# Token layout of the split moving operands: even and odd tokens of each block of 256 stored apart

## The reference

```python
def _swiglu(x, w_in, w_out):                      # D_FF = 2816, four times
    a, b = jnp.split(x @ w_in, 2, axis=-1)
    return (jax.nn.silu(a) * b) @ w_out
...
z = n @ mix_w_in[l]                               # per layer of the first stack
merged = jax.nn.sigmoid(zga) * (y_a @ proj_a[l]) + jax.nn.sigmoid(zgb) * (y_b @ proj_b[l])
h = h + mod[:, 1, 2] * (merged @ w_out[l])
...
def sq_relu_mlp(h, w_in, w_out):                  # width 4096, three times
    return jnp.square(jax.nn.relu(h @ w_in)) @ w_out
...
qkv = h @ w_qkv                                   # second stack, layer 1
o_lat = o_blocks.transpose(1, 0, 2, 3, 4, 5).reshape(B, L, D) @ w_o
```

## Time and profile before

| | before |
|---|---|
| median of three runs | 3466.84 us |
| range of the runs | 3464.92 to 3466.95 us |
| span of the profiled execution | 3464.7 us |
| TensorE matmul busy | 3413.6 us, 18,494 records |
| TensorE weight loads busy | 2874.5 us |
| VectorE busy | 2165.7 us |
| ScalarE busy | 1318.4 us |
| GpSimd busy | 298.0 us |
| DMA | 452.01 MB, mean 130 GB/s |

### The profile page before, as it was taken

How to read it: one execution, slowest core, us unless ns; L and a number is a source line. 1 busy time by engine, 2 the same in 40 slices (tenths; PEclk the granted TensorE clock), 3 DMA queues, 4 the chain that set the end, 5 groups by cost and what they waited for, 6 DMA issues and landing times.

```text
span 3464.7 us, 46915 instructions
## 1 busy us (share of the span) xinstructions
PE 3413.6 (99%) x18494; PEld 2874.5 (83%) x18494; DVE 2165.7 (63%) x3570; ACT 1318.4 (38%) x1951; POOL 298.0 (9%) x376
## 2 busy tenths in 40 slices
PE   9999999999999999999999999999999999999998
PEld 7888967898888988896789888899988898588888
DVE  7555565656555655666577777888776556655444
ACT  4222463333222422245333523355533236643222
POOL 0000232001000100023100000012100001210000
PEclk9999999999999999999999999999999999999999
DMA  7444302434444344320243444344444311013221
GB/s 279 188 158 163 107 24 101 163 129 168 158 162 151 134 169 158 148 106 12 101 164 140 149 150 170 146 147 182 172 174 165 117 66 68 25 50 112 96 98 48
DMA packets 85561, 452.01 MB, mean 130 GB/s; under 512 B 10304, under 2 KB 12544, under 8 KB 48608
## 3 DMA queue, kind: packets, MB, share of 16 engines
q1 hardware_dynamic: 83168, 439.10, 34.2%
q0 software_dynamic: 2176, 9.92, 0.8%
HBM read 446.88 MB, written 2.10 MB: 130 GB/s over the span
## 4 chain that ended last, share of the span: by engine, by line
PE 84%; DVE 7%; ACT 3%; issue 2%; DMA 2%; POOL 0%; SPq 0%; DVEq 0%; ACTq 0%; POOLq 0%
PE ps L662 21%; PE ps L663 21%; PE ps L664 21%; DVE WL L568 2%; DMA araw<-in_ast 2%; PE ps L2778 1%; PE ps L2780 1%; PE ps L2779 1%; PE ps L3477 1%; PE ps L1039 1%; PE ps L1040 1%; PE ps L1041 1%; ACT P L1859 1%; PE ps L1776 1%; PE ps L1299 1%
## 5 line engine op out<-in xcount | busy, mean ns | idle before, releaser
L662 PE MATMUL ps<-nH,WH 128*128 128x512 f32 x2256 | 880.3, 390 | 0.4 <-ACT rot L3207 0.4
L664 PE MATMUL ps<-nH,WL 128*128 128x512 f32 x2256 | 877.8, 389 | 0.0
L663 PE MATMUL ps<-nL,WH 128*128 128x512 f32 x2256 | 877.8, 389 | 0.0
L568 DVE TENSOR_TENSOR WL<-raw,WH 128x2048 fp32r<-128x2048 f32 (+2 forms) x297 | 651.6, 2199 | 361.5 <-ACT WH L557 360.0
L557 ACT ACTIVATE WH<-raw 128x2048 fp32r<-128x2048 f32 (+2 forms) x299 | 543.2, 1822 | 561.1 <-PE ps L664 479.9
L662 PEld LDWEIGHTS ps<-nH,WH 128*128 128x128 f32 x2256 | 423.5, 188 | 90.6 <-issue 3.3
L664 PEld LDWEIGHTS ps<-nH,WL 128*128 128x128 f32 x2256 | 423.4, 188 | 88.3
L663 PEld LDWEIGHTS ps<-nL,WH 128*128 128x128 f32 x2256 | 423.5, 188 | 87.2 <-issue 0.2
L628 DVE SCALAR_TENSOR_TENSOR araw<-araw,cB 128x1024 f32<-128x1024 f32 x224 | 275.6, 1230 | 205.6 <-DMA araw<-in_ast 205.2
L662 PE MATMUL ps<-hH,WH 128*128 128x512 f32 x944 | 368.8, 391 | 2.5 <-DVE ma L2454 1.4
L664 PE MATMUL ps<-hH,WL 128*128 128x512 f32 x944 | 367.4, 389 | 0.0
(11 more groups left out here) (452 smaller groups left out, 5940.0 us busy)
## 6 DMA issues: line engine op xcount, KB each, us to landing
raw<-in_wst SPq DMA_DIRECT2D x273, 1024.0 KB, 4.8
araw<-in_ast SPq DMA_DIRECT2D x225, 512.0 KB, 5.7
raw<-in_wst SPq DMA_DIRECT2D x18, 512.0 KB, 3.3
araw<-in_wst SPq DMA_DIRECT2D x9, 1024.0 KB, 4.8
row<-in_ast SPq DMA_DIRECT2D x15, 512.0 KB, 10.5
cw<-in_cw POOLq DMA_DIRECT2D x4, 1024.0 KB, 5.9
h<-in_xT SPq DMA_DIRECT2D x4, 512.0 KB, 5.6
raw<-in_wst SPq DMA_DIRECT2D x8, 256.0 KB, 2.6
```

The source lines that it names most:

```text
L568: dve.q.tensor_tensor(M.WL[k % NW][:, 0:n], M.raw[raw_use[k]][:, 0:n], M.WH[k % NW][:, 0:n].bitcast(F32), ALU.subtract).then_inc(*v_wlo.up(k))
L662: pe.q.matmul(to, hi[:, i, cc], xh, start=i == 0, stop=False)
L663: pe.q.matmul(to, hi[:, i, cc], xl, start=False, stop=False)
L664: t = pe.q.matmul(to, lo[:, i, cc], xh, start=False, stop=i == nk - 1)
```

## The change

Four views of a tile row are added. `blocks` and `in_turn` are for a tile in the new layout, `tokens` and `apart` for one in the old. In the new layout each block of 256 columns holds the 128 even tokens first and the 128 odd tokens behind them, so two neighbouring tokens lie 128 columns, 512 bytes, apart.

```diff
+def in_turn(t):
+    return t.rearrange("p (x a b) -> p x b a", a=2, b=128)
+
+def tokens(t):
+    return t.rearrange("p (x b a) -> p x b a", a=2, b=128)
+
+def apart(t):
+    return t.rearrange("p (x b a) -> p x a b", a=2, b=128)
+
+def blocks(t):
+    return t.rearrange("p (x a b) -> p x a b", a=2, b=128)
```

```diff
@@ norm_act
-                act.q.activation(p.nH[:, i, 0:p.N], p.scr[i % 2][:, 0:p.N], ACT.Identity, scale=G[:, i:i + 1],
-                                 bias=shift[:, i:i + 1]).then_inc(*a_xhi.up(g, i))
+                act.q.activation(in_turn(p.nH[:, i, 0:p.N]), tokens(p.scr[i % 2][:, 0:p.N]), ACT.Identity,
+                                 scale=G[:, i:i + 1], bias=shift[:, i:i + 1]).then_inc(*a_xhi.up(g, i))
@@ norm_dve
-                dve.q.tensor_tensor(p.nL[:, i, 0:N], p.scr[2 + i % 2][:, 0:N], p.nH[:, i, 0:N].bitcast(F32),
+                dve.q.tensor_tensor(blocks(p.nL[:, i, 0:N]), apart(p.scr[2 + i % 2][:, 0:N]), blocks(p.nH[:, i, 0:N].bitcast(F32)),
                                     ALU.subtract).then_inc(*v_xlo.up(g, i))
@@ normed_x
-            return (lambda i: (p.nH[:, i, 0:p.N], p.nL[:, i, 0:p.N])), (lambda i: (a_xhi.to(g, i), v_xlo.to(g, i)))
+            return (lambda i: (in_turn(p.nH[:, i, 0:p.N]), in_turn(p.nL[:, i, 0:p.N]))), (lambda i: (a_xhi.to(g, i), v_xlo.to(g, i)))
@@ ffn_pe
-                    slot_pair(pe, w_out, N, lambda i: (hH[:, ci % 2, i, :], hL[:, ci % 2, i, :]),
+                    slot_pair(pe, w_out, N, lambda i: (in_turn(hH[:, ci % 2, i, :]), in_turn(hL[:, ci % 2, i, :])),
@@ the last slots of a feed-forward block, in halves of 256 tokens
-                    xh, xl = M.hH[:, ci % 2, f, c], M.hL[:, ci % 2, f, c]
+                    xh, xl = in_turn(M.hH[:, ci % 2, f, c]), in_turn(M.hL[:, ci % 2, f, c])
...
```

More of the change, by code:

```diff
@@ L1323, in group @@
                 pe.wait_ge(*v_wlo.to(k))
-                products(pe, k, o % 2, KT, b[:, 0:S // 2], lambda i: (M.mH[:, i, c], M.mL[:, i, c]),
+                products(pe, k, o % 2, KT, b[:, 0:S // 2], lambda i: (in_turn(M.mH[:, i, c]), in_turn(M.mL[:, i, c])),
                          lambda i: (a_hhi.to(g, "m", i), v_hlo.to(g, "m", i)), (g, "O", x, o), free)
@@ L1344, in four @@
                             pe.wait_ge(*v_hlo.to(g, "m", i))
[L1345 to L1349 removed]
+                            xh, xl = in_turn(M.mH[:, i, c]), in_turn(M.mL[:, i, c])
+                            pe.q.matmul(to[o], hi[:, i, cc], xh, start=i == 0, stop=False, skip_group_check=True)
+                            pe.q.matmul(to[o], hi[:, i, cc], xl, start=False, stop=False, skip_group_check=True)
+                            t = pe.q.matmul(to[o], lo[:, i, cc], xh, start=False, stop=i == 7, skip_group_check=True)
                         if i == 7:
@@ L1523, in low @@
                 dve.wait_ge(*a_xhi.to(g, i))
-                dve.q.tensor_tensor(lat.nL[:, i, :], lat.scr[2 + i % 2][:, :], lat.nH[:, i, :].bitcast(F32), ALU.subtract
+                dve.q.tensor_tensor(blocks(lat.nL[:, i, :]), apart(lat.scr[2 + i % 2][:, :]), blocks(lat.nH[:, i, :].bitcast(F32)), ALU.subtract
                                     ).then_inc(*v_xlo.up(g, i))
@@ L2041, in out1_dve @@
             dve.wait_ge(*a_yhi.to(g, ft))
-            dve.q.tensor_tensor(M.yaL[:, ft, :], lat.scr[2 + ft % 2][:, :], M.yaH[:, ft, :].bitcast(F32), ALU.subtract
+            dve.q.tensor_tensor(blocks(M.yaL[:, ft, :]), apart(lat.scr[2 + ft % 2][:, :]), blocks(M.yaH[:, ft, :].bitcast(F32)), ALU.subtract
                                 ).then_inc(*v_ylo.up(g, ft))
@@ L2803, in second @@
                             pe.wait_ge(*v_hlo.to(g, ci, i // 2 * 2))
-                            t = three(to, k, i, slice(c * 128, c * 128 + 128), M.hHc[:, ci % 2, i, :], M.hLc[:, ci % 2, i, :],
-                                      ci == i == o % 2 == 0, ci == CHUNKS2 - 1 and i == 3)
+                            t = three(to, k, i, slice(c * 128, c * 128 + 128), in_turn(M.hHc[:, ci % 2, i, :]),
+                                      in_turn(M.hLc[:, ci % 2, i, :]), ci == i == o % 2 == 0, ci == CHUNKS2 - 1 and i == 3)
                         if o == 7 or o % 2 and ci == CHUNKS2 - 1:
@@ L2863, in hidden @@
                 dve.wait_ge(*a_hhi.to(g, ci, f))
-                dve.q.tensor_tensor(M.hLc[:, ci % 2, f:f + 2, :], y[:, :].rearrange("p (a b) -> p a b", a=2),
-                                    M.hHc[:, ci % 2, f:f + 2, :].bitcast(F32), ALU.subtract).then_inc(*v_hlo.up(g, ci, f))
+                dve.q.tensor_tensor(blocks(M.hLc[:, ci % 2, f:f + 2, :].rearrange("p f c -> p (f c)")), apart(y[:, :]),
+                                    blocks(M.hHc[:, ci % 2, f:f + 2, :].rearrange("p f c -> p (f c)").bitcast(F32)),
+                                    ALU.subtract).then_inc(*v_hlo.up(g, ci, f))
             for ci in range(CHUNKS2):
@@ L3619, in part @@
                     pe.wait_ge(*v_ylo.to("y2", i))
-                    pe.q.matmul(to, hi[:, i, cc], lat.nH[:, i, c], start=i == 0, stop=False, skip_group_check=True)
-                    pe.q.matmul(to, hi[:, i, cc], lat.nL[:, i, c], start=False, stop=False, skip_group_check=True)
-                    t = pe.q.matmul(to, lo[:, i, cc], lat.nH[:, i, c], start=False, stop=i == 7, skip_group_check=True)
+                    xh, xl = in_turn(lat.nH[:, i, c]), in_turn(lat.nL[:, i, c])
+                    pe.q.matmul(to, hi[:, i, cc], xh, start=i == 0, stop=False, skip_group_check=True)
+                    pe.q.matmul(to, hi[:, i, cc], xl, start=False, stop=False, skip_group_check=True)
+                    t = pe.q.matmul(to, lo[:, i, cc], xh, start=False, stop=i == 7, skip_group_check=True)
                 if tiles[-1] == 7:
```

64 lines of the change are left out of this document (30 added, 34 removed).

## The result

The changed kernel takes 3356.26 us, the median of four runs (3355.71 to 3358.09), against 3466.89 us for the kernel before beside it (3464.92 to 3469.53). The ratio is 0.968, with a 95% interval of 0.967 to 0.970: 110.6 us faster, where 148 were forecast.

The account below looks back on a forecast made before the run. TensorE's matmul stream was taken to bound the kernel. Savings of 110, 42 and 11 us make 163, less 15 lost: 148 off the 3464.7 us span, 3316.7, plus 2.1 to the median: 3319 us; range 3290 to 3557.

Parts of the forecast that it names:

- Bound and pace: TensorE's matmul stream sets the time; 512-wide products go from 226.7 to 215.8 ns, 110 us over 10,128.
- the surplus: Time of a float32r matmul over one column per 2.4 GHz tick: 13.3 ns, expected to fall to 2.5 at width 512.
- the likeliest case: Whole kernel: the matmul surplus gone or most of it, 3290 to 3400 us, chance 0.66.
- The floor of the 256-wide products: Weight loads keep 256-wide products at 110.3 ns, down from 120.0: 42 us for 4,320, plus 11 us for context.
- The reason: In TensorE's matmuls, moving and weight reads collide; two slow streams should behave like the float32 pass, 2.5 ns over.
- Half rate: Rival: float32r columns from two places need two accesses, so products fall to float32 pace, 429.2 ns; 6083 us, chance 0.15.
- ScalarE's writes: High parts jumping 512 bytes per element: taken as nothing; far end 128 us of ScalarE work, 9 us uncovered.
- VectorE's reads: Low parts reading one input at every second element: costed at nothing, far end nothing too, after copy L1891.
- What is not cashed: Matmul gain lost to loads at 2484 to 2664 us (9 us) and VectorE at 2200 to 2400 (6 us): 15 us.

Follow-up runs that it names:

- the pad: Kernel before with the pad tile 8 words wide instead of 24, moving right-side tiles by 64 bytes: 3476.92 us against 3465.75.
- b=4: Changed kernel with blocks of 8 tokens instead of 256, neighbouring tokens 16 bytes apart: 3355.98 us, one run.
- b=2: Changed kernel with blocks of 4 tokens instead of 256, neighbouring tokens 8 bytes apart: 3464.21 us, one run.
- b=128: Layout of the changed kernel itself, blocks of 256 tokens, neighbouring tokens 512 bytes apart, against the kernel before: 3356.26 us.
- b=64: Changed kernel with blocks of 128 tokens instead of 256, neighbouring tokens 256 bytes apart: 3354.62 us, one run.

## Why the prediction was right, and where it failed

**Bound and pace: right.** TensorE's stream set the time (79% of the chain, 97% busy), the surplus went, and 3356 us lies in the likeliest case's own range, 3290 to 3400, 37 us above the forecast. The step from 226.7 to 215.8 ns came out as 215.83, 110 us for 10,128 products as forecast.

**The floor of the 256-wide products: 1.3 ns too low.** I took 110.3 ns from 3.53 us / 32. That divides a piece of the chain that doesn't hold the run from start to start. The timeline of before, once for the whole run and once for its first four:

```profile
460.20 0.55 PE L1641 MATMUL ps<-R,cw 128*128 128x62 f32 x4
...
460.20 3.68 PE L1641 MATMUL ps<-R,cw 128*128 128x62 f32 x32
```

The 28 that follow take (3.68 - 0.55) / 28 = 111.8 ns each; to the nanosecond the distances in the trace are 111 and 112, with an average of 111.7 behind a first one of 56. That is just what the 256-wide products run at now, 5.0 ns over their columns and not 2.5. Against my 110.3 ns that is 1.3 x 5,856 = 8 us. That the loads of weights are what sets it stays an inference. The matmuls' gain was thus about 155 us and not 163.

**The reason: only half of it held.** "The moving operand's read and the weights' read get in each other's way" agrees with the step-2 weights (13.3 to 20.0 ns) and with the pad. "Two streams at the slow pace should behave as the float32 pass does" fell: `b=4` has no slow streams and no surplus, `b=2` has it. What the runs show in its place is a rule with no mechanism: the surplus goes if each column comes from another 16-byte piece than the one before it. The forecast had the right number from the wrong picture, and that the surplus of the float32 pass, 2.5 ns, came back here is luck as far as the runs can tell.

**Half rate: refuted.** One tick served one column in every layout tried. The Trainium skill ("Advanced Engine Details and Errata", SBUF Cachelines) has lines of 16 bytes, at least two hits on one needed, and a penalty for a different line at each access. For the moving operand the measurement says the opposite: a different piece at each column runs at 215.8 ns, and the straight read, with four hits on each, at 226.7. For ScalarE's writes the rule fits: 633 ns with hits in the same piece (`b=2`), 1152 without.

**ScalarE's writes: the term was mis-sized and the cover too.** "The low end is no change, the high end a second 0.83 ns": it is (1156 - 633) / 512 = 1.02 ns per element with TensorE reading straight, so the truth lay beyond the far end, and I had taken the near one, from a copy on another engine. I kept 9 us on the path as the far end. The cost in time is known from the pairs: writing straight gives 9.0 us back with blocks of 256 and 19.8 with blocks of 8, and leaving out all of the writers' change 17.6 us. So of 122 us more work on ScalarE about a seventh reached the end.

**VectorE's reads: "nothing as the far end too" failed.** They cost 138 ns per low part. The row I leaned on, L1891, is at 669 ns in the changed kernel, as cheap as before, and it runs there beside 512-wide products that read in turn, at 399 to 418 us and at 1469 to 1488. So a read with a step beside such products is not enough for the price: the subtraction has a second operand, and which of the differences counts no run tells. What the runs do show is that it takes TensorE's reads in turn and a wide layout (`b=128` and `b=64`, not `b=4`). No row of before could show it. The mean of 669 (673 before) also hides two kinds, twelve copies of some 590 ns and four of some 920, so "the same per element" was read from a mixture. In time the miss cost nothing that the runs show.

**What is not cashed: the right places, too little.** For 2484 to 2664 us I counted the whole 9 us as lost, and the changed kernel gains 0.2 us there (88.1 us ahead at its end, 87.9 to 88.0 at its start). For 2200 to 2400 us I kept 6 of 12; it loses 1.7 us (from 87.0 to 85.3 ahead). With only the reads changed the two give 2.0 and 1.2 us. The kernel with only the reads gains 127.2 us (3465.85 - 3338.64) of some 155, so even without the writers' cost about 28 us were lost where I had 15. Its trace accounts for them: 18.2 us more idle time of TensorE than before (69.3 and 51.1) and 42.0 us at the lower clock where before had 25.2, which is 8.4 us. That is 26.6 us, for the most part VectorE late by one to six microseconds at single places, and TensorE at half speed behind some of them. The clock I had not counted at all.

The sum, in the order of the prediction: 163 - 8 for the floor, - 26.6 for waits and clock without the writers' cost, - 17.6 for the writers is 110.8 us, and 110.6 were measured. The 17.6 is itself a difference of measured times; the 155 and the 26.6 are worked out from the traces.

## What to carry to other kernels

Measure the distance between the starts of matmuls in a dense stretch and compare it with columns per tick: a constant over it that changes with the tile was a matter of the reads here, and it fell from 13.3 to 2.5 ns at width 512, and to 5.0 at 256, once neighbouring columns came from different 16-byte pieces. Choose the smallest layout that does this (blocks of 8 tokens here), and look at what it costs those who write it: ScalarE should read apart and write straight on. When TensorE gets 5% faster, look for the stretches where another engine is already late by a microsecond here and there. In the one here VectorE was busy for 76% on average, four waits of 0.8 to 1.5 us stood in it, and it gained nothing.

## What the runs showed of the hardware

- A float32r product whose columns come from alternating 16-byte pieces runs at 512 columns in 215.8 ns, whatever tile it reads; straight reads have 226.7, and 226, 229 or 232 by the pair of tiles after a shift of 64 bytes.
- Reading the weights at a step of 2 made the straight-read product slower, 233.3 ns.
- ScalarE pays 1.0 ns per element for writes that change the 16-byte piece each time, and for a read at every second element 878 ns per 512 with `b=128`, 680 with `b=4`, against 633. The first of these needs no TensorE in turn beside it (1156 ns), the second was only measured with it.
- VectorE's subtraction with one operand read apart in blocks of 256 took 825 ns while TensorE read in turn and 688 while it read straight. The Trainium skill ("SBUF — State Buffer", Who interferes with whom) has one source of contention alone, the ports that VectorE and GpSimd share, and reads of TensorE apart from them; these two runs, in which none of the 152 subtractions overlaps a record of GpSimd, speak against that for such patterns.
- The granted clock went down to 1.2 GHz ten times in the changed kernel and four before. In the changed kernel each time follows an idle time of TensorE of 1.1 to 5.9 us, but other idle times of up to 2.4 us have none behind them.

What stays open: why the 16-byte piece decides, and whether it is the aligned piece, what sets the surplus of a straight read at a given address, and whether two columns per piece are enough. Results written in turn into PSUM from straight tiles, which would spare the writers altogether, were not tried.
